# Feed-forward and MLP first products: the high and the low weights' matmuls alternate

## What is computed

```
def conv_ffn(x, w_in, conv_w, conv_b, w_out):
    gate, up = jnp.split(x @ w_in, 2, axis=-1)
    ...
    h = jax.nn.gelu(gc) * up
    return h @ w_out

def sq_relu_mlp(h, w1, w2):
    u = jax.nn.relu(h @ w1)
    return (u * u) @ w2
```

## Time and profile before

| | us |
|---|---|
| median of 3 runs | 1351.08 |
| lowest, highest | 1350.56, 1352.66 |
| profiled execution, first to last instruction | 1352.2 |
| PE busy in it | 1316.8 |
| PEld busy | 1136.4 |
| DVE busy | 936.7 |
| ACT busy | 656.0 |

### The profile page before, as it was taken

One profiled execution on the slowest core, in us unless ns is written; L12 is line 12 of the kernel. 1 busy time (PEld: TensorE's weight loads), 2 busy tenths in 40 slices (PEclk: granted clock), 3 DMA queues, 4 the chain that ended last, 5 costly groups with the idle time before them and its releaser, 6 DMA issues.

```text
span 1352.2 us, 23686 instructions
## 1 busy us (share of the span) xinstructions
PE 1316.8 (97%) x9424; PEld 1136.4 (84%) x9424; DVE 936.7 (69%) x1636; ACT 656.0 (49%) x1008; POOL 104.5 (8%) x106
## 2 busy tenths in 40 slices
PE   8999999999999999999999998999999999999999
PEld 6887897888888888888888887888888888888887
DVE  6684256777777865877777588766666796676664
ACT  4332323644444776644444577543334568544431
POOL 0002344000000020000000010000001042000000
PEclk9899999999999999999999999999999999999999
DMA  9632112655552332755551550884531422573610
GB/s 248 201 121 87 65 66 63 219 188 190 192 193 91 106 125 92 238 190 192 191 186 63 187 186 2 300 306 160 213 125 63 164 102 86 206 287 137 242 63 32
DMA packets 111272, 208.51 MB, mean 154 GB/s; under 512 B 3920, under 2 KB 53456, under 8 KB 110672
## 3 DMA queue, kind: packets, MB, share of 16 engines
q1 hardware_dynamic: 111184, 207.28, 44.8%
HBM read 206.21 MB, written 1.05 MB: 153 GB/s over the span
## 4 chain that ended last, share of the span: by engine, by line
PE 87%; DVE 6%; ACT 5%; issue 1%; POOL 0%; DMA 0%; SPq 0%; DVEq 0%; ACTq 0%; POOLq 0%
PE ps L1041 21%; PE ps L988 18%; PE ps L893 11%; PE ps L993 10%; PE ps L1114 2%; PE ps L1083 2%; PE ps L1225 2%; PE ps L1449 2%; PE ps L1357 1%; PE ps L964 1%; ACT Ah L1895 1%; DVE Al L2702 1%; PE ps L1493 1%; PE ps L817 1%; PE ps L852 1%
## 5 line engine op out<-in xcount | busy, mean ns | idle before, releaser
L988 PE MATMUL ps<-hTx,Ah 128*128 128x512 f32 x1088 | 270.7, 391 | 0.0
L2709 DVE TENSOR_TENSOR Al<-ringA,Ah 128x2048 fp32r<-128x2048 f32 x74 | 169.3, 2287 | 97.2 <-ACT Ah L1905 97.2
L988 PEld LDWEIGHTS ps<-hTx,Ah 128*128 128x128 f32 x1088 | 199.7, 188 | 38.5
L993 PEld LDWEIGHTS ps<-hTx,Al 128*128 128x128 f32 x1152 | 156.7, 190 | 10.6
L1940 ACT COPY xn<-ps 128x512 f32<-128x512 f32 x72 | 42.3, 587 | 244.1 <-PE ps L993 236.9
L993 PE MATMUL ps<-hTx,Al 128*128 128x256 f32 x1152 | 160.7, 282 | 0.0
L1905 ACT CAST Ah<-ringA 128x2048 fp32r<-128x2048 f32 x76 | 145.8, 1918 | 13.1 <-PE ps L893 10.3
L1914 ACT CAST Bh<-ringB 128x1024 fp32r<-128x1024 f32 (+1 forms) x76 | 107.1, 1409 | 89.5 <-PE ps L1041 89.5
L893 PE MATMUL ps<-Ah,hTx 128*128 128x512 f32 (+1 forms) x576 | 136.5, 387 | 2.8 <-ACT Ah L1895 1.4
L2716 DVE TENSOR_TENSOR Bl<-ringB,Bh 128x1024 fp32r<-128x1024 f32 (+1 forms) x76 | 127.0, 1670 | 10.6 <-ACT Bh L1914 10.2
L1041 PE MATMUL ps<-Bh,hidh 128*128 128x512 f32 x416 | 129.9, 392 | 1.1 <-issue 1.1
(11 more groups left out here) (446 smaller groups left out, 2066.5 us busy)
## 6 DMA issues: line engine op xcount, KB each, us to landing
ringA<-in_ffn_w_in SPq DMA_DIRECT2D x44, 1024.0 KB, 7.1
ringA<-in_mlp_w SPq DMA_DIRECT2D x32, 1024.0 KB, 7.4
ringB<-in_mlp_w SPq DMA_DIRECT2D x32, 1024.0 KB, 6.8
ringB<-in_ffn_w_out SPq DMA_DIRECT2D x44, 512.0 KB, 4.2
ringA<-in_diff_w_in SPq DMA_DIRECT2D x12, 1024.0 KB, 6.8
ringA<-in_dsa_w_in SPq DMA_DIRECT2D x8, 1024.0 KB, 7.2
ringA<-in_w_k SPq DMA_DIRECT2D x4, 1024.0 KB, 13.0
ringA<-in_w_r SPq DMA_DIRECT2D x4, 1024.0 KB, 9.5
```

The lines of the kernel that those rows point to most:

```text
L988: mm(o.rearrange("p (i t) -> p i t", i=2), w_hi, hTx[:, :, k * T:(k + 1) * T], start=(k == 0), stop=False)
L993: last = mm(o[:, T:2 * T], Al[:, half, k * T + j * P:k * T + j * P + P], hTh[:, k, :], start=False, stop=(k == KT - 1))
L2709: V.tensor_tensor(a_split(w, Al, half), a_half(w, (a_at[w] + par) % 2, half), a_split(w, Ah, half).bitcast(F32), ALU.subtract).then_inc(al ...
```

## The change

In `first` the order of the matmuls of one feature block changes. Before, the eight 512-column matmuls with the high weights come first and the eight 256-column ones with the low weights behind them. Now the two alternate: for each `k` the 512-column one and then the 256-column one. Their sums in PSUM hold the same terms. PE waits for `al_rdy` ahead of the first matmul of the half. Chunk 0 and the last half (`single`) keep the order of before (`behind`).

```
+                    pe.wait_ge(ah_rdy, ch * 2 + (S0[w] + half + 1))
+                    behind = single or (isinstance(ch, int) and ch == 0)
+                    if not behind:
+                        pe.wait_ge(al_rdy, ch * 2 + (S0[w] + half + 1))
                     for j in range(2):
                         o = ps[:, 4 + 2 * half + j, :]
-                        if j == 0:
-                            pe.wait_ge(ah_rdy, ch * 2 + (S0[w] + half + 1))
+
+                        def low(k):
+                            return mm(o[:, T:2 * T], Al[:, half, k * T + j * P:k * T + j * P + P],
+                                      hTh[:, k, :], start=False, stop=(k == KT - 1))
+
                         for k in range(KT):
...
                                 mm(o.rearrange("p (i t) -> p i t", i=2), w_hi,
                                    hTx[:, :, k * T:(k + 1) * T], start=(k == 0), stop=False)
-                        if j == 0:
-                            pe.wait_ge(al_rdy, ch * 2 + (S0[w] + half + 1))
-                        for k in range(KT):
-                            last = mm(o[:, T:2 * T], Al[:, half, k * T + j * P:k * T + j * P + P],
-                                      hTh[:, k, :], start=False, stop=(k == KT - 1))
+                                if not behind:
+                                    last = low(k)
+                        if behind:
+                            if j == 0:
+                                pe.wait_ge(al_rdy, ch * 2 + (S0[w] + half + 1))
+                            for k in range(KT):
+                                last = low(k)
```

## The result

The changed kernel takes 1355.87 us (median of 7 runs, 1354.39 to 1358.38) against 1351.23 us for the kernel before, measured with it (median of 7 runs, 1350.56 to 1352.66). The ratio is 1.0035, with a 95% interval of 1.0024 to 1.0045: slower, by 4.6 us. The forecast was 1350.3 us, a change too small to measure, and that was wrong; the time lies within the range given, on the side of rival C.

A forecast was written before the change was run, and what follows sets the result against it. The prediction took PE's matmul pace, without waits, to bound the kernel. Steady prices gain 0.8 us over 64 halves and the earlier wait costs nothing: 1350.3 us on the median, range 1342 to 1357 us.

The forecast's parts named there:

- rival C: In alternating halves the pace never settles: 5 to 9 ns per long matmul, 4.3 to 8.4 us lost; chance 0.25.
- What bounds the kernel: In both loops PE never waits, busy 141.21 of 141.21 us and 132.32 of 132.32; its pace sets the time.
- The earlier wait: Ahead of a changed half PE waits for the low weights 1.81 us sooner, claimed to cost nothing.
- The price of a pair: In changed halves, one 512-column plus one 256-column matmul was to cost 346.7 ns, against 347.5 before.
- the steady sum: For each alternating pair, the steady-run prices added: 226.7 + 120 = 346.7 ns, a gain of 0.8 us over 64 halves.
- first-contact prices: At a change of width: short behind long 113 ns, long behind short some 233, together 346 to 347 ns.
- the quick short matmul: The first 256-column matmul behind a 512-column one takes about 113 ns, 7 less than steady.
- Rival B: In changed halves every short matmul gets its quick first price: 340 ns a pair, 1343.5 us; chance 0.27.
- The rule weighed in the prediction: Weight loads take about 107 ns for 128 columns, so a short matmul gains most from a long neighbour, favouring 340 ns.
- The sum sets a span: For the whole kernel: the profiled span of 1352.2 us less 0.8 gives 1351.4; on the median of runs 1350.3 us.
- A: Same pace in changed halves: 344.5 to 349 ns a pair, time within 2.7 us, likeliest 1350.3; chance 0.46.

The follow-up runs named there:

- the groups of two: Against the kernel before, two 512-column matmuls alternate with two 256-column ones in each changed half; ratio 1.0005 (0.9993 to 1.0016).
- the tail version: Against the kernel before, a half runs fourteen 512-column matmuls, fourteen 256-column ones, then two and two; 1348.32 against 1351.16 us, ratio 0.9979.
- groups of four: Against the kernel before, four 512-column matmuls alternate with four 256-column ones in each changed half; ratio 1.0021 (1.0010 to 1.0031).
- with 384 columns alternating: The changed kernel with the low weights' matmul 384 columns wide, leaving out 64 tokens; 9.23 us a half with its second product.
- groups of eight: The same 512 and 384 column widths, in eights instead of alternating at every matmul; 9.25 us a half with its second product.

## Why the prediction was wrong, point by point

- **What bounds the kernel** was right: PE's pace in the loops, with no waits. Nothing but PE's busy time moved.
- **The earlier wait at no cost** was right: the run with the wait alone shows it.
- **The price of a pair** failed: "I take the steady sum. The two first-contact prices point to it". The sum had 346.7 ns a pair; measured are 353.3 in the middle of a half and 5.64 us for its 16 pairs (8.387 less 2.75 for the second product, which takes what it took in the earlier trace rows), 352.5 on average. The first intervals were measured behind settled runs of eight, where a long matmul stands behind seven more short ones and a short one behind seven more long ones. I took them as properties of the contact between two matmuls. They are not: of the three pairs that recur, one costs 0.11 + 0.23 us, near my sum, and two cost 0.12 + 0.24.
- **Rival C** was the right mechanism. Its lowest price, 4.3 us by 5 ns for each long matmul, comes close to the 4.6 us measured, but by luck: in the three pairs that recur the long ones take about 236 ns (0.24, 0.24 and 0.23 us), some 10 more than steady and beyond C's highest price of 9, and the short ones about 117, 3 less than the 120 that C gave them. The evidence named for it was on record ("some five long matmuls that are longer" after each change of width), and in an alternating order every matmul stands within those five. It should have been the forecast. What I held against it, that the quick short matmul gives back 7 ns, holds in full for one pair in three.
- **Rival B** has the right price for the short matmul in that one pair only (113 ns), and inside the alternation the long ones never came down to 226.7.
- **The rule weighed in the prediction**, by which the short product gains most from a long neighbour, came true in its sign alone: the short ones gained 3 ns on average, and the long ones lost some 10, for which it has no term. That a long matmul pays because its weights are loaded behind a short one is refuted by the groups of two.
- **Two slips** change nothing in the forecast. The sum sets a span (1352.2 us) beside the median of the runs; a span is shorter than its run's time, by 1.8 us in the changed kernel's profile. And A's 344.5 to 349 ns a pair come to 3.1 us less to 1.5 us more than before, not to 2.7 us either way.

What stays open is why the pace after a change of width takes the values it takes. It is exact: by the starts in the trace the first product of each of the 64 halves of the changed kernel takes 5.640 us, whatever DVE, ACT and the transfers do meanwhile. It is no function of the number of changes: against before a half gains 0.013 us in groups of two (15 changes of width in its 32 matmuls), loses 0.047 in groups of four (7) and 0.080 alternating (31), and the tail version, with three changes like the kernel before, gains 0.033. For long runs, and for a tail like one already seen, the measured intervals add up to within 0.01 us a half; for new short patterns nothing here predicts them.

## What to carry to other kernels

Matmuls of different widths are not independent prices where PE is the bound. The order to try first is whole products by width, and not by the loop that they come from: here it gained 0.11%, and its price could be worked out beforehand. Fewer changes of width are no rule, though: by the traces groups of two were quicker than groups of four and of eight, and with 384 columns alternating was quicker than groups of eight. Read a pattern's price from that pattern, from the starts of consecutive matmuls, and where the trace shows a transient behind each change, cost an order that changes everywhere by the transient and not by the steady state. A reordering that neither adds nor removes work can still move the time in both directions, here by +0.35% and -0.21%.

## What the runs showed of the hardware

In the rows below the 13 ns on top of the stream are there only at the higher clock. They are of the kernel before: two windows with the granted clock (the last number but two, 0.50 and 1.00) and the timeline of 256-column matmuls in both:

```profile
47.50:52.50 5.00, 5.00 (x25) 5.00 (x25) 4.66 (x17) 3.81 (x5) 0.00 (x0) 0.50 0.10 37
54.00:58.00 4.00, 4.00 (x36) 4.00 (x35) 3.62 (x7) 0.59 (x1) 0.00 (x0) 1.00 0.41 112
```

```profile
47.12 2.04 PE L1225 MATMUL ps<-kxh,kwh 128*128 128x256 f32 x8 [2.88 <-issue]
48.96 1.91 PE L1225 MATMUL ps<-kxl,kwh 128*128 128x256 f32 x8
50.67 1.91 PE L1225 MATMUL ps<-kxh,kwl 128*128 128x256 f32 x8
...
53.61 1.12 PE L1225 MATMUL ps<-kxl,kwh 128*128 128x256 f32 x8
54.57 1.12 PE L1225 MATMUL ps<-kxh,kwl 128*128 128x256 f32 x8
```

PE had been idle for 2.88 us before the slower ones and worked without a break into the quicker ones. At 1.2 GHz eight matmuls take 1.71 us, 213.8 ns each, which is 256 columns at that clock (213.3 ns) and next to nothing more; at 2.4 GHz 0.96 us, 120 ns each, 13.3 over the stream. Half the clock costs these matmuls 1.78 times and not twice the time. What the 13 ns are, and whether they have to do with the unsettled pace, no run here shows.
